# The narrow columns of a projection made with its first value block, in column groups of 296

## The chip, the cores and the metric

One core of one Trainium2 chip. The time is device microseconds of one execution; runs of the kernel before gave 530.16, 530.44 and 530.63 us, median 530.44. Lower is better.

## What is computed

A block of a streaming encoder, for 256 tokens of 2048 features, in float32. `h = RMSNorm(x)`; one projection `proj = h @ w_in` with 9296 columns, split into `qa ka va ga qb kb vb gb` (1024 columns each), `qi` (1024), and the two narrow ones: `ki` (64 columns, the indexer's key) and `wi` (16 columns, the indexer's head weights). Mixer A is chunked attention with a learned bias. Mixer B scores every key with an indexer,

```
logits = einsum('bqhd,bsd->bqhs', qi, ki);  score = einsum('bqh,bqhs->bqs', wi * idx_scale, relu(logits))
```

keeps the 64 best admissible keys of each query, and attends to these. Both outputs are gated by `silu(g)`, projected by `w_out`, added to `x`, and normed once more.

## The kernel before

Each float32 operand is split into a high part in the `f32r` format and the rest in the same format (`w_hi`, `w_lo`; `a_hi`, `a_lo`), and a product is made of three passes on TensorE: hi x hi, lo x hi, hi x lo. The RMS norm's scale is applied when results leave PSUM, so TensorE starts on `x * gain` before the sums of squares exist.

The weights stream in units of 256 rows (UK = 2 tiles k of 128) by 512 columns (512 KB) through a ring of four slots. For each unit the queue of SyncE (SP) issues a load once VectorE (DVE) has finished with the slot (`lo_done`), ScalarE (ACT) makes the high part (`split_hi`, L667 to 674) once TensorE (PE) has finished with the slot (`mm_done`), DVE the low part (`split_lo`, L956 to 961), and PE multiplies. 8 units are a block, 22 blocks the kernel. All orders are written out by hand, one instruction stream per engine.

There are two kinds of block. A token-major block (`unit`, L395) holds activations stationary and streams 512 weight columns: 96 matmuls of 512 columns, into two 512-column banks of `acc`, one for each tile m of 128 tokens. A feature-major block (`feature_unit`, L410) holds weights stationary and streams tokens: pairs of a matmul over hi and lo activations together (L426) and one with the low weights (L424 or L429). In blocks 1 and 2 it uses 192 of the 256 tokens, so the pairs are of 384 and 192 columns.

The stage that matters, in PE's order (L433 to L514): eight matmuls on zeros while the first loads fly; block 0, which is token-major and makes 512 columns of `va`, at first in halves of a unit (L442 to L479), each one k, so that PE can start early; units 0 to 2 of block 1 (feature-major, `qi`); the sums of squares, as matmuls with ones (L487 to L490); unit 3; the narrow columns, 80 of them stationary, 256 tokens moving, three passes for each of 16 k (L494 to L497) into `aux[0]`; a wait until block 0's result has left `acc` (`both_out(1)`, L499); units 4 and 5; three transposes that turn the narrow result token-major (L504 to L508); units 6 and 7; and two transposes of `ki_nat` (L512), which is the key normed and doubled. Block 2 (L542) then begins to need the indexer's keys.

The narrow weights, 640 KB, are one load (L301) with its own split (L734 on ACT, L1053 on DVE) into tiles `nw_raw`, `nw_hi`, `nw_lo`; the latter two serve later as scratch for attention. ACT squares the activations after its eighth split (L717 to L731), DVE adds them up between its low parts (L1034 to L1051), then makes the rates 1/rms per token in two layouts, `rstd` and `rk` (L1056 to L1062). `block_out` (L676 on ACT, L963 on DVE) takes block 0's result out of `acc`. On the queue of ACT lie the loads of the first activations and of the gain (L691, L692), on SP's the rest (L288 to L304).

Of the kernel before, what the change touches and what calls it, by code (L numbers as in the profile page):

```python
# [26 lines left out]
NARROW = IDX_D + IDX_H  # L27
QT = T - CHUNK
# [12 lines left out]
UK = 2  # L41
# [5 lines left out]
def hybrid_block(nc, xT, x, norm_gain, w_blocks, w_narrow, rel_bias, wo_blocks, final_gain, out):  # L47
# [7 lines left out]
    with ExitStack() as ctx:  # L55
# [10 lines left out]
        w_raw = sb("w_raw", [P, RING, UK * CB])  # L66
        w_hi = sb("w_hi", [P, RING, UK, CB], f32r)
        w_lo = sb("w_lo", [P, RING, UK, CB], f32r)
        nw_raw = sb("nw_raw", [P, KT * NARROW])
        nw_hi = sb("nw_hi", [P, KT, NARROW], f32r)  # L70
        nw_lo = sb("nw_lo", [P, KT, NARROW], f32r)
# [17 lines left out]
        narrow = sb("narrow", [NARROW, T])  # L89
        narrow_twice = sb("narrow_twice", [NARROW, P])  # L90
# [20 lines left out]
        idx_rate0 = sb("idx_rate0", [P, 1])  # L111
# [35 lines left out]
        nw_landed = sem("nw_landed")  # L147
# [16 lines left out]
        nhi_done = sem("nhi_done")  # L164
        nlo_done = sem("nlo_done")
# [5 lines left out]
        narrow_done = sem("narrow_done")  # L171
# [61 lines left out]
        AUX0_INDEX, AUX0_PAIRS = 2, 10  # L233
        AUX1_INDEX, AUX1_PAIRS = 2, 6
# [11 lines left out]
        w_hi4 = w_hi[:, :, :, :].rearrange("p r k c -> p r (k c)").rearrange("p r (k c) -> p r k c", k=2 * UK)  # L246
        w_lo4 = w_lo[:, :, :, :].rearrange("p r k c -> p r (k c)").rearrange("p r (k c) -> p r k c", k=2 * UK)

        nhi_flat, nlo_flat = flat(nw_hi[:, :, :]), flat(nw_lo[:, :, :])
# [21 lines left out]
        SCALAR_PART = slice(1408, D)  # L271

# [4 lines left out]
        def _(sp):  # L277
# [23 lines left out]
            sp.dma_start(nw_raw[:, :], w_narrow).then_inc(nw_landed, 16)  # L301
# [34 lines left out]
        def _(pool):  # L336
# [30 lines left out]
            pool.wait_ge(narrow_done, 1)  # L367
# [298 lines left out]
        def _(act):  # L666
# [33 lines left out]
            for u in range(HALVED):  # L700
                for kk in range(UK):
# [5 lines left out]
                    if k > 0:  # L707
                        a_part(k)
# [753 lines left out]
```

## Time and profile before

| | |
|---|---|
| median of three runs | 530.44 us (530.16 to 530.63) |
| the profiled execution's own time | 529.62 us |
| its span, first to last instruction | 527.6 us |
| PE busy | 519.2 us, 98% of the span |
| DVE, ACT, POOL busy | 366.7, 273.8, 29.8 us |
| granted TensorE clock | 0.997 of full speed |
| first matmul on data | 5.32 us |
| first matmul of block 1 | 27.67 us |
| first transpose of `ki_nat` | 52.73 us |

The span is what the trace covers; the time of an execution has some 2 us more around it. Times of single instructions are microseconds from the start of the span. A matmul's duration overlaps the next one's, so the price of a matmul in a stream is the distance from its start to the next start.

### The profile page before, as it was taken

The numbers are of one execution on the slowest core, as the hardware profiler recorded it, in microseconds if no ns is written. First come the engines' busy times: TensorE is split into PE (matmuls) and PEld (weight loads), VectorE is DVE, ScalarE is ACT, GpSimd is POOL, SyncE is SP. The second block draws the span as 40 slices with busy tenths as digits, with TensorE's granted clock in tenths as the row PEclk, the third lists the DMA queues.
The fourth block names the chain that finished last, engine by engine and source line by source line (L and its number), as shares of the span: only waits on it lengthen the run. The fifth ranks groups of instructions, "written<-read, shape, count | busy, mean of one in ns | idle before, by whom it ended". The sixth has DMA issues, their size and how long they took to land.

```text
span 527.6 us, 8251 instructions
## 1 busy us (share of the span) xinstructions
PE 519.2 (98%) x2871; PEld 451.9 (86%) x2871; DVE 366.7 (70%) x551; ACT 273.8 (52%) x405; POOL 29.8 (6%) x46
## 2 busy tenths in 40 slices
PE   9999999999999999999999999999999999999994
PEld 6899998888888888888888888888888888888883
DVE  6898685665668766767676767586877887646454
ACT  6875544444543344445554637374655566434342
POOL 1005043150000000000000000000000000000000
PEclk9999999999999999999999999999999999999998
DMA  8966966658555555563746454645555775665614
GB/s 298 381 205 187 288 203 214 196 174 279 172 190 196 197 199 183 182 196 106 234 145 194 148 176 157 191 147 183 159 160 176 252 250 170 189 198 194 202 44 159
DMA packets 72668, 102.53 MB, mean 194 GB/s; under 512 B 3504, under 2 KB 61760, under 8 KB 72384
## 3 DMA queue, kind: packets, MB, share of 16 engines
q1 hardware_dynamic: 70944, 96.68, 56.7%
q0 software_dynamic: 1264, 5.00, 3.0%
q10 hardware_dynamic: 432, 0.47, 0.3%
q8 instruction: 19, 0.31, 0.2%
q14 instruction: 9, 0.07, 0.1%
HBM read 99.24 MB, written 2.11 MB: 192 GB/s over the span
## 4 chain that ended last, share of the span: by engine, by line
PE 98%; DVE 0%; ACT 0%; DVEq 0%; issue 0%
PE acc L426 38%; PE acc L424 18%; PE acc L391 11%; PE acc L392 11%; PE acc L393 11%; PE acc L429 1%; PE aux L496 1%; PE acc L457 1%; PE aux L585 1%; PE aux L606 1%; PE acc L439 1%; PE aux L611 0%; PE aux L583 0%; PE aux L612 0%; PE aux L613 0%; PE aux L527 0%
## 5 line engine op out<-in xcount | busy, mean ns | idle before, releaser
L426 PE MATMUL acc<-acts,w_hi 128*128 128x512 f32 (+1 forms) x896 | 304.8, 389 | 0.0
L960 DVE TENSOR_TENSOR w_lo<-w_raw,w_hi 128x1024 fp32r<-128x1024 f32 x172 | 213.2, 1244 | 107.3 <-ACT w_hi L674 106.0
L674 ACT ACTIVATE w_hi<-w_raw 128x1024 fp32r<-128x1024 f32 x172 | 181.7, 1058 | 156.8 <-PE acc L426 81.9
L424 PE MATMUL acc<-acts,w_lo 128*128 128x256 f32 (+1 forms) x840 | 232.8, 277 | 0.0
L426 PEld LDWEIGHTS acc<-acts,w_hi 128*128 128x128 f32 x896 | 166.5, 188 | 30.1
L424 PEld LDWEIGHTS acc<-acts,w_lo 128*128 128x128 f32 x840 | 158.6, 189 | 1.0
L391 PE MATMUL acc<-w_hi,acts 128*128 128x512 f32 x248 | 96.6, 389 | 0.0
L392 PE MATMUL acc<-w_lo,acts 128*128 128x512 f32 x248 | 96.5, 389 | 0.0
L393 PE MATMUL acc<-w_hi,acts 128*128 128x512 f32 x248 | 96.5, 389 | 0.0
L391 PEld LDWEIGHTS acc<-w_hi,acts 128*128 128x128 f32 x248 | 46.6, 188 | 10.0 <-issue 0.3
L392 PEld LDWEIGHTS acc<-w_lo,acts 128*128 128x128 f32 x248 | 46.6, 188 | 9.6
L393 PEld LDWEIGHTS acc<-w_hi,acts 128*128 128x128 f32 x248 | 46.6, 188 | 9.6
L689 ACT ACTIVATE low<-acc 128x512 f32<-128x512 f32 (+1 forms) x28 | 16.0, 570 | 15.8 <-PE acc L426 15.8
L989 DVE TENSOR_TENSOR qk<-acc,low 128x512 f32<-128x512 f32 (+1 forms) x16 | 11.0, 687 | 9.2 <-ACT low L689 9.2
L383 POOL DMA_DIRECT2D qk<-x x1 | 0.5, 533 | 296.2 <-PE aux L585 296.2
L826 ACT ACTIVATE p<-p,neg_top,q_rate 128x256 f32<-128x256 f32 (+1 forms) x16 | 8.6, 537 | 15.9 <-DVE neg_top L1256 15.9
L429 PE MATMUL acc<-acts,w_lo 128*128 128x256 f32 (+1 forms) x56 | 15.5, 277 | 0.0
L829 ACT ACTIVATE p<-p,neg_max 128x256 f32<-128x256 f32 (+1 forms) x16 | 7.1, 444 | 11.8 <-DVE neg_max L1252 11.8
L924 ACT ACTIVATE t_gate<-z 128x512 f32<-128x512 f32 x8 | 5.0, 627 | 15.3 <-DVE z L1386 15.3
L835 ACT ACTIVATE nw_hi<-aux 128x512 fp32r<-128x512 f32 x8 | 4.8, 598 | 14.6 <-PE aux L597 14.6
L429 PEld LDWEIGHTS acc<-acts,w_lo 128*128 128x128 f32 x56 | 10.5, 188 | 1.1
L1129 DVE SCALAR_TENSOR_TENSOR iscore<-relu,w_idx,iscore 128x256 f32<-128x256 f32 x16 | 11.0, 688 | 0.3
(179 smaller groups left out, 388.1 us busy)
## 6 DMA issues: line engine op xcount, KB each, us to landing
w_raw<-w_blocks SPq DMA_DIRECT2D x140, 512.0 KB, 3.6
w_raw<-wo_blocks SPq DMA_DIRECT2D x32, 512.0 KB, 4.3
w_raw<-w_blocks SPq DMA_DIRECT2D x8, 256.0 KB, 5.3
qk<-x POOLq DMA_DIRECT2D x1, 2048.0 KB, 10.7
qk<-xT SPq DMA_DIRECT2D x7, 256.0 KB, 6.0
o<-ext_dram POOLq DMA_DIRECT2D x1, 1024.0 KB, 8.1
fgain<-final_gain POOLq DMA_DIRECT2D x1, 1024.0 KB, 7.8
out<-o SPq DMA_DIRECT2D x2, 512.0 KB, 3.0
```

The source lines that it names most:

```text
L391: nc.tensor.matmul(dst, a_hi[:, k, t], hi, start=start, stop=False)
L392: nc.tensor.matmul(dst, a_hi[:, k, t], lo, start=False, stop=False)
L393: return nc.tensor.matmul(dst, a_lo[:, k, t], hi, start=False, stop=stop)
L424: nc.tensor.matmul(acc[:, bank:bank + n], w_lo4[:, u % RING, q, c], a_hi[:, k, tokens], start=False, stop=False)
L426: last = nc.tensor.matmul(whole, w_hi4[:, u % RING, q, c], acts[:, k, :, tokens], start=(k == 0), stop=(k == KT - 1))
L429: nc.tensor.matmul(acc[:, bank:bank + n], w_lo4[:, u % RING, q, c], a_hi[:, k, tokens], start=False, stop=False)
L674: nc.scalar.activation(flat(w_hi[:, s, :, :]), w_raw[:, s, :], ACT.Copy).then_inc(hi_done, 1)
L689: nc.scalar.activation(low[:, half, :, 0:n], parts[:, :, n:2 * n], ACT.Copy).then_inc(low_out, 1)
L826: last = nc.scalar.activation(p[:, h, :], p[:, h, :], ACT.Exp, bias=neg_top[:, t, h:h + 1], scale=q_rate[:, 1 - t:2 - t], accum_out=p_sum[ ...
L960: nc.vector.tensor_tensor(flat(w_lo[:, s, :, :]), w_raw[:, s, :], flat(w_hi[:, s, :, :]).bitcast(f32), ALU.subtract).then_inc(lo_done, 1)
L989: nc.vector.tensor_tensor(dst, parts[:, :, 0:T], low[:, half, :, :], ALU.add).then_inc(feat_out, 1)
L1129: nc.vector.scalar_tensor_tensor(iscore1[:, :], relu1[:, h, :], w_idx1[:, head:head + 1], iscore1[:, :], ALU.mult, ALU.add).then_inc((isum ...
```

## The change

The 80 narrow columns are no longer a product of their own. They are appended to block 0's 512 columns: 592 columns for each k, made token-major as two groups of 296. The first group goes to `acc`, the second to `aux[0]` and `aux[1]` (for the two tiles of tokens), and holds the last 216 columns of `va` and the 80 narrow ones. The ring's slots are widened to 2 x 592 columns; other blocks use the first 1024 columns of a slot. The tiles `nw_raw`, `nw_hi`, `nw_lo`, `narrow` and `narrow_twice` go, and so do the 48 narrow matmuls and the three transposes. The scratch that later stages kept in `nw_hi` and `nw_lo` is now `parts_hi` and `parts_lo`.

The loads: 80 columns of two k are a load for each unit, with 320 bytes in a run; the first is on ACT's queue, the others ahead of their unit's weights on SP's. The first k's weights come in two pieces (296 and 216 columns), and are split and multiplied in two pieces. The sums of squares follow unit 0 of block 1 instead of unit 2; ACT and DVE make the squares and their sum correspondingly sooner, and `rstd` before `rk`. DVE reads the narrow columns directly from `aux`, just after it took the values out, and the transposes of `ki_nat` come after unit 5 instead of unit 7.

Loads, and PE's part:

```diff
+            def load_narrow(u):
+                sp.dma_start(raw_slots[:, u % RING, :].rearrange("p (k c) -> p k c", k=UK)[:, :, CB:WIDE],
+                             w_narrow[:, u * UK * NARROW:(u + 1) * UK * NARROW].rearrange("p (k c) -> p k c", k=UK)
+                             ).then_inc(nw_landed[u % RING], 16)
+
             for u in range(HALVED):
-                sp.dma_start(w_raw[:, u, 0:CB], w_blocks[VA_FIRST, u, :, 0:CB]).then_inc(half_landed[u], 16)
                 if u == 0:
+                    sp.dma_start(raw_slots[:, 0, 0:PART], w_blocks[VA_FIRST, 0, :, 0:PART]).then_inc(first_landed, 16)
+                    sp.dma_start(raw_slots[:, 0, PART:CB], w_blocks[VA_FIRST, 0, :, PART:CB]).then_inc(half_landed[0], 16)
                     sp.dma_start(xT_land[:, 1, :], xT[:, 1, :]).then_inc(xT_landed[0], 16)
-                sp.dma_start(w_raw[:, u, CB:2 * CB], w_blocks[VA_FIRST, u, :, CB:2 * CB]).then_inc(w_landed[u], 16)
+                else:
+                    load_narrow(u)
+                    sp.dma_start(raw_slots[:, u, 0:CB], w_blocks[VA_FIRST, u, :, 0:CB]).then_inc(half_landed[u], 16)
+                sp.dma_start(raw_slots[:, u, WIDE:WIDE + CB], w_blocks[VA_FIRST, u, :, CB:2 * CB]
+                             ).then_inc(w_landed[u], 16)
                 k = slice(UK * (u + 1), UK * (u + 2))
                 sp.dma_start(xT_land[:, k, :], xT[:, k, :]).then_inc(xT_landed[u + 1], 16)
             for u in range(HALVED, UNITS):
                 sp.wait_ge(lo_done, u - RING + 1)
-                load(u, w_blocks[VA_FIRST, u, :, :])
+                load_narrow(u)
+                sp.dma_start(raw_slots[:, u % RING, :].rearrange("p (k c) -> p k c", k=UK)[:, :, 0:CB],
+                             w_blocks[VA_FIRST, u, :, :].rearrange("p (k c) -> p k c", k=UK)
+                             ).then_inc(w_landed[u % RING], 16)
                 if u + 1 < UNITS:
                     k = slice(UK * (u + 1), UK * (u + 2))
                     sp.dma_start(xT_land[:, k, :], xT[:, k, :]).then_inc(xT_landed[u + 1], 16)
-            sp.dma_start(nw_raw[:, :], w_narrow).then_inc(nw_landed, 16)
...
+            def wide_pass(k, part, a, w, start=False, stop=False):
+
+                c = (k % UK) * WIDE + part * PART
                 for m in range(TM):
+                    dst = (acc[:, m * CB:m * CB + PART], aux[m][:, 0:PART])[part]
+                    last = nc.tensor.matmul(dst, a[:, k, m * P:m * P + P], w[:, (k // UK) % RING, c:c + PART],
+                                            start=start, stop=stop)
+                return last
...
+            wide_pass(0, 1, a_hi, lo_slots)
 
             for k in range(1, 2 * UK):
                 pe.wait_ge(ahi_done, k)
                 pe.wait_ge((half_hi, hi_done)[k % UK], k // UK + 1)
-                early_k(k, a_hi, w_hi)
+                for part in range(2):
+                    wide_pass(k, part, a_hi, hi_slots)
                 pe.wait_ge(alo_done, k + 1)
-                early_k(k, a_lo, w_hi)
+                for part in range(2):
+                    wide_pass(k, part, a_lo, hi_slots)
                 pe.wait_ge((half_lo, lo_done)[k % UK], k // UK + 1)
-                last = early_k(k, a_hi, w_lo)
...
+            for u in range(2, UNITS):
+                if u >= HALVED:
+                    pe.wait_ge(alo_done, UK * u + UK)
+                    pe.wait_ge(lo_done, u + 1)
                 for kk in range(UK):
                     k = u * UK + kk
-                    pe.wait_ge(alo_done, k + 1)
-                    pe.wait_ge((half_lo, lo_done)[kk], u + 1)
-                    for m in range(TM):
-                        last = mm3(acc[:, m * CB:m * CB + CB], k, m, w_hi[:, u, kk, :], w_lo[:, u, kk, :],
-                                   False, False)
+                    if u < HALVED:
+                        pe.wait_ge(alo_done, k + 1)
+                        pe.wait_ge((half_lo, lo_done)[kk], u + 1)
+                    for n, (a, w) in enumerate(((a_hi, hi_slots), (a_hi, lo_slots), (a_lo, hi_slots))):
+                        for part in range(2):
+                            last = wide_pass(k, part, a, w, stop=(k == KT - 1 and n == 2))
                 last.then_inc(mm_done, 1)
-            for u in range(HALVED, UNITS):
-                pe.wait_ge(alo_done, UK * u + UK)
-                unit(0, u)
-            for u in range(3):
-                feature_unit(1, u, 1, CHUNK)
+            feature_unit(1, 0, 1, CHUNK)
             pe.wait_ge(cleared, 3 + HEADS)
             pe.wait_ge(summed, UNITS)
             nc.tensor.matmul(aux[2][:, 0:T], ones_mat[:, :], x_sum[:, 0:T], start=True, stop=True)
             for m in range(TM):
                 last = nc.tensor.matmul(aux[3][:, m:m + 1], x_sum[:, m * P:m * P + P], ones[:, :], start=True, stop=True)
             last.then_inc(ssq_made, 1)
-            feature_unit(1, 3, 1, CHUNK)
-
-            pe.wait_ge(nlo_done, 1)
-            for k in range(KT):
-                for n, (w, a) in enumerate(((nw_hi, a_hi), (nw_hi, a_lo), (nw_lo, a_hi))):
-                    last = nc.tensor.matmul(aux[0][0:NARROW, 0:T], w[:, k, :], a[:, k, :],
-                                            start=(k == 0 and n == 0), stop=(k == KT - 1 and n == 2))
-            last.then_inc(narrow_done, 1)
+            for u in range(1, 4):
+                feature_unit(1, u, 1, CHUNK)
             both_out(1)
             feature_unit(1, 4, 1, CHUNK)
             feature_unit(1, 5, 1, CHUNK)
             pe.wait_ge(patterned, 1)
-            pe.wait_ge(aux_read[0], 1)
-            for m in range(TM):
-                nc.tensor.transpose(aux[1][:, m * P:m * P + NARROW], narrow[:, m * P:m * P + P],
-                                    ident[0:NARROW, 0:NARROW])
-            nc.tensor.transpose(aux[1][:, TM * P:TM * P + NARROW], narrow_twice[:, :],
-                                ident[0:NARROW, 0:NARROW]).then_inc(narrow_done, 1)
-            feature_unit(1, 6, 1, CHUNK)
-            feature_unit(1, 7, 1, CHUNK)
-            pe.wait_ge(aux_read[1], 2)
+            pe.wait_ge(aux_read[1], 1)
             for m in range(TM):
                 last = nc.tensor.transpose(aux[0][:, m * P:m * P + P], ki_nat[:, m, :], ident[:, :])
             last.then_inc(kit_done, 1)
+            feature_unit(1, 6, 1, CHUNK)
+            feature_unit(1, 7, 1, CHUNK)
```

ACT and DVE:

```diff
+            act.dma_start(raw_slots[:, 0, :].rearrange("p (k c) -> p k c", k=UK)[:, :, CB:WIDE],
+                          w_narrow[:, 0:UK * NARROW].rearrange("p (k c) -> p k c", k=UK)).then_inc(nw_landed[0], 16)
...
+                    c = WIDE_K[kk]
+                    if k == 0:
+                        act.wait_ge(first_landed, 16)
+                        nc.scalar.activation(hi_slots[:, 0, 0:PART], raw_slots[:, 0, 0:PART],
+                                             ACT.Copy).then_inc(first_hi, 1)
+                        c = slice(PART, WIDE)
                     act.wait_ge((half_landed, w_landed)[kk][u], 16)
+                    if kk == 0:
+                        act.wait_ge(nw_landed[u], 16)
...
             split_lo(0, 8)
-            for u in range(1, 4):
+            for u in range(1, 3):
                 add_square(u)
             split_lo(0, 9)
+            add_square(3)
             add_square(4)
-            add_square(5)
             split_lo(0, 10)
-            add_square(6)
-            split_lo(0, 11)
-            add_square(7)
+            for u in range(5, UNITS):
+                add_square(u)
             dve.wait_ge(summed, UNITS - 1)
             nc.vector.tensor_tensor(x_sum[:, 0:T], x_sum[:, 0:T], x_sum[:, T:2 * T], ALU.add).then_inc(summed, 1)
...
+            split_lo(0, 11)
             dve.wait_ge(ssq_made, 1)
```

DVE's order after that: `ssq`, `rk` (scaled), `split_lo(0, 12)`, `rstd`, the two rates, the values out of `acc` and `aux` in two pieces each (`acc_out` is given after the pieces of `acc`), `wi` and `ki_nat` from `aux`, `split_lo(0, 13)`, and then the reciprocals of `rk` and `q_rate`. ACT's: splits 8 to 12 with the squares, the roots of `ssq` and `rk`, the values in two pieces, split 13.

## Rows read from the trace of the kernel before

**Rows 1.** The page's busy times and chain: us (share) xinstructions; shares by engine.

```profile
PE 519.2 (98%) x2871; PEld 451.9 (86%) x2871; DVE 366.7 (70%) x551; ACT 273.8 (52%) x405; POOL 29.8 (6%) x46
...
PE 98%; DVE 0%; ACT 0%; DVEq 0%; issue 0%
```

**Rows 2.** Waits of PE over the span: us in total, times, longest.

```profile
PE acc L436 <- DVE ki_bd L998: 1.1, 1, 1.1
```

**Rows 3.** Timeline of PE, block 0: start us, us, what.

```profile
5.32 1.29 PE L444 MATMUL acc<-w_hi,acts 128*128 128x512 f32 x4
...
16.70 0.47 PE L391 MATMUL acc<-w_hi,acts 128*128 128x512 f32 x1
17.02 0.39 PE L392 MATMUL acc<-w_lo,acts 128*128 128x512 f32 x1
...
27.67 0.33 PE L426 MATMUL acc<-acts,w_hi 128*128 128x384 f32 x1
```

**Rows 4.** Chain of waits, 0 to 60 us: start, us, what.

```profile
34.77 0.43 PE aux L487 x2
...
37.93 5.58 PE aux L496 x48
```

**Rows 5.** Timeline of PE around the three transposes, block 1.

```profile
47.71 0.37 PE L426 MATMUL acc<-acts,w_hi 128*128 128x384 f32 x1
...
48.09 0.33 PE L424 MATMUL acc<-acts,w_lo 128*128 128x192 f32 x1
48.26 0.36 PE L426 MATMUL acc<-acts,w_hi 128*128 128x384 f32 x1
```

**Rows 6.** Timeline of PE, matmuls of 256 columns in a row (attention scores).

```profile
236.63 0.28 PE L581 MATMUL aux<-nw_hi 128*128 128x256 f32 x1
...
237.34 0.27 PE L585 MATMUL aux<-qk,q_early 128*128 128x128 f32 x1
```

**Rows 7.** Timeline of PE, a pair of 384 and 192 columns.

```profile
28.32 0.36 PE L426 MATMUL acc<-acts,w_hi 128*128 128x384 f32 x1
28.52 0.25 PE L424 MATMUL acc<-acts,w_lo 128*128 128x192 f32 x1
28.61 0.37 PE L426 MATMUL acc<-acts,w_hi 128*128 128x384 f32 x1
```

**Rows 8.** Timeline of all engines, the start.

```profile
4.91 0.35 DVE L1003 TENSOR_SCALAR acts<-qk,gain 128x256 fp32r<-128x256 f32 x1 [3.48 <-DMA gain<-norm_gain]
6.83 0.51 ACT L696 ACTIVATE acts<-qk,gain 128x256 fp32r<-128x256 f32 x1 [0.81 <-DMA qk<-xT]
...
14.24 1.06 ACT L674 ACTIVATE w_hi<-w_raw 128x1024 fp32r<-128x1024 f32 x1 [0.28 <-DMA w_raw<-w_blocks]
```

**Rows 9.** Issues of DMAs: KB each, us to landing.

```profile
gain<-norm_gain ACTq DMA_DIRECT2D x1, 8.0 KB, 3.7
```

**Rows 10.** DMA queues, 0 to 5, 5 to 20, 20 to 45 us: packets, MB, share of 16 engines.

```profile
q10 hardware_dynamic: 288, 0.14, 11.2%
...
q1 hardware_dynamic: 2472, 5.80, 102.7%
...
q1 hardware_dynamic: 5345, 5.49, 69.2%
```

**Rows 11.** Groups of DVE and of ACT, to 28 us: busy us, mean ns.

```profile
L1018 DVE TENSOR_TENSOR w_lo<-w_raw,w_hi 128x512 fp32r<-128x512 f32 x8 | 5.5, 689 | 0.4 <-ACT w_hi L710 0.4
L960 DVE TENSOR_TENSOR w_lo<-w_raw,w_hi 128x1024 fp32r<-128x1024 f32 x6 | 7.3, 1225 | 1.8 <-ACT w_hi L674 1.8
...
L710 ACT ACTIVATE w_hi<-w_raw 128x512 fp32r<-128x512 f32 x8 | 5.0, 626 | 1.6 <-DMA w_raw<-w_blocks 1.5
```

**Rows 12.** Timeline of DVE: three sums of squares, the last sum, values out.

```profile
25.45 2.28 DVE L1038 TENSOR_TENSOR o<-o 128x512 f32<-128x512 f32 x3
...
33.78 0.43 DVE L1051 TENSOR_TENSOR o<-o 128x256 f32<-128x256 f32 x1
...
41.28 0.75 DVE L966 TENSOR_SCALAR v<-acc,rstd 128x512 f32<-128x512 f32 x1
```

More of the change, by code:

```diff
@@ L27 @@
 NARROW = IDX_D + IDX_H
+WIDE = CB + NARROW
+PART = WIDE // 2
+V_REST = CB - PART
 QT = T - CHUNK
@@ L146, in hybrid_block @@
         xT_landed = [sem(f"xT_landed{c}") for c in range(UNITS)]
-        nw_landed = sem("nw_landed")
+        first_landed = sem("first_landed")
+        nw_landed = [sem(f"nw_landed{s}") for s in range(RING)]
         gain_landed = sem("gain_landed")
@@ L673, in split_hi @@
                     act.wait_ge(mm_done, g * UNITS + (c - RING + 1))
-                nc.scalar.activation(flat(w_hi[:, s, :, :]), w_raw[:, s, :], ACT.Copy).then_inc(hi_done, 1)
+                nc.scalar.activation(hi_slots[:, s, 0:UK * CB], w_raw[:, s, :], ACT.Copy).then_inc(hi_done, 1)
             def block_out(g, dst):
@@ L1066, in _ @@
                                            ALU.mult).then_inc(rated, 1)
-            dve.wait_ge(rated, 2)
+            dve.wait_ge(mm_done, UNITS)
+            nc.vector.tensor_scalar(v1_flat[:, V_COLUMNS[0]], acc[:, CB:CB + PART], rstd[:, 1:2], None,
+                                    ALU.mult).then_inc(acc_out[1], 1)
+            nc.vector.tensor_scalar(v1_flat[:, V_COLUMNS[1]], aux[1][:, 0:V_REST], rstd[:, 1:2], None, ALU.mult)
+            dve.wait_ge(v_hi_done, 1)
+            for part, (c, src) in enumerate(zip(V_COLUMNS, (acc[:, 0:PART], aux[0][:, 0:V_REST]))):
+                last = nc.vector.scalar_tensor_tensor(v0_lo_flat[:, c], src, rstd[:, 0:1], v0_hi_flat[:, c].bitcast(f32),
+                                                      ALU.mult, ALU.subtract)
+                if part == 0:
+                    last.then_inc(acc_out[0], 1)
+            dve.wait_ge(rated, 2)
+            nc.vector.tensor_scalar(w_early[:, :], aux[0][:, V_REST + IDX_D:PART], idx_rate[:, 0:1], None,
+                                    ALU.mult).then_inc(w_scaled, 1)
+            nc.vector.tensor_scalar(w_idx1[:, :], aux[1][:, V_REST + IDX_D:PART], idx_rate[:, 1:2], None, ALU.mult)
+            for m in range(TM):
+                for h in range(2):
+                    last = nc.vector.tensor_scalar(ki_nat[:, m, h * IDX_D:(h + 1) * IDX_D],
+                                                   aux[m][:, V_REST:V_REST + IDX_D], rstd[:, m:m + 1], None, ALU.mult)
+            last.then_inc(aux_read[1], 1)
+            dve.wait_ge(w_scaled, 1)
+            for f in range(2):
+                nc.vector.tensor_copy(w_idx0[rows[f], :, :],
+                                      w_early[CHUNK:P, :].rearrange("p (i f h) -> p i f h", i=4, f=2)[:, :, f, :])
+            split_lo(0, 13)
+            dve.wait_ge(std_done, 2)
+            nc.vector.reciprocal(rk[:, :], rk[:, :]).then_inc(rk_made, 1)
             nc.vector.reciprocal(q_unit[:, :], q_rate[:, :]).then_inc(rated, 1)
-            for h in range(2):
-                nc.vector.tensor_copy(idx_rate0[rows[h], :], idx_rate[CHUNK:P, 0:1]).then_inc(rated, 1)
-            split_lo(0, 13)
-            block_out(0, 1, slice(2 * CB, 3 * CB))
             split_lo(0, 14)
@@ L1082, in _ @@
             split_lo(0, 17)
-            dve.wait_ge(rated, 5)
-            dve.wait_ge(narrow_done, 2)
-            early_w = aux[1][:, TM * P + IDX_D:TM * P + NARROW].rearrange("p (i f h) -> p i f h", i=4, f=2)
-            for f in range(2):
-                nc.vector.tensor_scalar(w_idx0[rows[f], :, :], early_w[rows[f], :, f, :], idx_rate0[rows[f], :], None,
-                                        ALU.mult)
-            nc.vector.tensor_scalar(w_idx1[:, :], aux[1][:, P + IDX_D:P + NARROW], idx_rate[:, 1:2], None, ALU.mult)
-            for m in range(TM):
-                for h in range(2):
-                    last = nc.vector.tensor_scalar(ki_nat[:, m, h * IDX_D:(h + 1) * IDX_D],
-                                                   aux[1][:, m * P:m * P + IDX_D], rstd[:, m:m + 1], None, ALU.mult)
-                last.then_inc(aux_read[1], 1)
-            split_lo(0, 18)
             dve.wait_ge(kit_done, 1)
```

123 lines of the change are left out of this document (64 added, 59 removed).

## The prediction, before the changed kernel was run

> **What bounds the kernel now.** I read the busy times and the chain first [rows 1]. PE is busy for 98% of the span and the chain that ended last runs on PE for 98% of it, while DVE, ACT and the queues have next to none. The list of PE's waits over the whole span has one entry, 1.1 us before any data is there [rows 2]. So a change pays exactly what it takes from PE's stream, and costs what it makes PE wait. No other engine's saving counts by itself. The timeline of PE then gives the price of each kind of matmul, as the distance from start to start.
>
> - 512 columns: block 0 is 96 matmuls. Its 50th starts at 17.02 us and block 1 starts at 27.67 [rows 3], which is 47 matmuls later, so 0.2266 us each.
> - 256 columns: six in a row from 236.63 to 237.34 [rows 6], 0.118 us each.
> - The 48 narrow matmuls, 80 columns stationary and 256 moving: 5.58 us [rows 4], 0.116 us each.
> - In block 1 a matmul of 384 columns holds the next one off for 0.20 us and one of 192 for 0.09 [rows 7].
>
> Block 0 takes 27.67 - 5.32 = 22.35 us [rows 3]; 96 x 0.2266 is 21.75, so 0.60 us of it are start-up: late operands in the first units, and at 16.70 a matmul that holds the next off for 0.32 instead of 0.23 after a late low part.
>
> **What goes.** Block 0, 22.35 us, and the narrow matmuls, 5.58 us. The three transposes: between a 384 matmul and the 192 after it lie 47.71 and 48.09, 0.38 us where 0.20 is usual, and the next start comes 0.17 later instead of 0.09 [rows 5, 7], together 0.26 us. Sum 28.19 us. The sums of squares (0.43 us and a little more, rows 4), the two transposes of `ki_nat` and all feature units stay in the stream and only change places: nothing on either side.
>
> **What comes.** 16 k x 3 passes x 2 token tiles x 2 groups = 192 matmuls of 296 columns. No row has 296 columns. The line through the points at 256 and 512 gives 0.118 + 40 x (0.2266 - 0.118)/256 = 0.135 us. Bounds from other rows: below, no less than the 256-column price, 0.118. Above, the line from 256 to the 384 columns of block 1, 0.118 + 40 x (0.20 - 0.118)/128 = 0.1436. I take 0.135: the straight line through 256 and 512 gives 0.172 at 384, so the 0.20 is a price of that mixed pair, and for a row of equal matmuls the evidence is the 256s and 512s. 192 x 0.135 = 25.92 us; by the bounds 22.7 and 27.6.
>
> **Start-up.** PE starts at 5.32 because `a_hi[0]` is made when the gain lands at 4.91 [rows 8]. That does not move, since gain and the first activations are issued first as before. The first piece of weights is smaller and lands no later than the 4.2 us of now, so that first pass is not late, but it was not what PE waited for: the two-piece load by itself brings at most a tenth or two. What is new is ACT's wait for the first narrow load before it may split the second piece. It is issued third on ACT's queue, 0.45 us behind the gain (from about 1.65), and with the gain's 3.7 us to landing [rows 9] it arrives at 5.4. Behind that waiting instruction on ACT are `a_hi[1]` and the high part of k 1, and DVE's second low piece follows it. ACT: second piece 5.4 to 5.85; `a_hi[1]` to 6.3; high part of k 1 (592 columns, 626 ns x 592/512 = 0.72, rows 11) to 7.0. PE meanwhile has group 0 (hi x hi), then waits for group 1 until 5.9, and goes through 12 matmuls to about 7.3. Unhindered they would have ended at 6.94. With some 0.3 us for the first matmuls, which today already come slower than the rest, I put the new start-up at 0.7 us beside the 0.60 now. Bounds: 0.3 if the load lands by 5.0, 1.8 if it lands at 6.5, where each tenth counts one for one.
>
> After that PE takes 12 x 0.135 = 1.62 us for a k and 3.24 for a unit, where it took 1.36 and 2.72. For a k, DVE needs 0.80 us for the low part (689 ns x 592/512, rows 11) and some 0.5 for the activations, ACT 0.72 and 0.51 [rows 8, 11]: both hidden. The DMA engines, full at 102.7% from 5 to 20 us [rows 10], are the nearer limit. Packets: 5.80 MB in 2472 packets at 102.7% of 15 us x 16 is 100 ns for 2.35 KB; 5.49 MB in 5345 at 69.2% of 25 x 16 is 52 ns for 1.03 KB; the line through both puts a packet of 320 B at 26 ns, the short packets of q10 at 31 ns on the mean [rows 10]. A unit's narrow part is 256 packets, so 256 x 26/16 = 0.42 us of all engines. Ahead of the weights of unit 4 lie five such loads, 2.1 us. Today they land at 14.24 [rows 8], then at 16.4; high part 1.23 us (1.06 x 1184/1024), low part 1.42 (1.225 x 1184/1024, rows 11), ready at 19.0. PE arrives at unit 4 at 5.32 + 0.7 + 4 x 3.24 = 18.98. So unit 4 has no slack at all, just as now, and a tenth or two of wait is within my 0.7. In the units before, the loads shift by 0.4 to 1.7 us (the activations of unit 1, waited for until 6.83 in rows 8, come at 7.3 or so; PE needs them at 9.2), and PE's slower pace covers that. From unit 5 on a unit's loads take 0.42 us longer than now and PE takes 0.52 us longer, so the queue keeps its place or gains.
>
> A rule of the Trainium skill speaks against these loads: "DMA: Bandwidth & Descriptors", under Specifications, asks for at least 512 B in a transfer for full rate and says that below it the engine reads, modifies and writes. The q10 row, where more than half of the packets are short, does not show that, but it holds no data packet between 64 and 1024 B. If a packet of 320 B cost twice as much, see the second rival.
>
> **Behind block 0.** Block 1 begins at 5.32 + 0.7 + 25.92 = 31.94. Unit 0 takes 8 x 0.289 = 2.31 us [rows 7], so PE wants the sum of squares at 34.25. ACT's split 10 waits for PE's seventh unit, 28.7, and ends at 29.8; DVE's low part to 31.0, three additions 2.28 us, the last one 0.43 [rows 12]: 33.7, ahead by 0.5 us. This is the shortest slack of the tail. Then both sums are on PE until 35.0. `rstd` waits on DVE behind low part 12 (1.22 us, from about 35.6 on), and is there at about 37; the values in two pieces for each tile, some 0.45 us for 296 columns by the 0.75 us for 512 [rows 12], let `acc` go by 38.6. PE reaches `both_out(1)` after three units of 2.31 us, at 41.9: 3 us of cover, where the narrow product gave it before. The reads of `ki_nat` and the head weights, seven short operations, lie before low part 13, which is then done at 41.2 and wanted at 44.2. `ki_nat`'s transposes at 46.6 find it ready and leave DVE more time before block 2 than now. POOL's removed wait was met long before the features it also waits for. From block 2 on nothing is different but the slots' pitch, and PE was never short there: the gain of the stage is kept to the end.
>
> **Sum.** 28.19 - (25.92 + 0.7) = 1.57 us. The profiled execution took 529.62 us around its span of 527.6: with the change 528.05. The median of the runs shown is 0.82 us higher than that execution, so on the median's scale 530.44 - 1.57 = 528.87, and I say 528.9.
>
> **Rivals.** (1) The 296-column matmul costs 0.1436 us, by the dearer line: 192 x 0.1436 = 27.57, and the gain is -0.1 us, time 530.5. For: block 1's rows show that smaller matmuls do not always follow the straight line. Against: 256 in a row cost 0.118, so 296 would have to leap. (2) Short packets cost double, 52 ns: 2.1 us more before unit 4, which then waits 2.1 us: gain -0.5, time 531.0. For: full DMA engines at that very place, and the rule named above. Against: q10's short packets at 31 ns. (3) Slower: the first narrow load lands very late. Its descriptors share the DMA engines with 1.2 MB on SP's queue, and loads behind a full queue have taken some 6 us. The mechanism is ACT's wait at the start, for which all splits queue up. It decides from a landing at 5.4 + 1.57 + 1.06 = 8.0 us on; at 8.3 the time is 530.44 - 1.57 + 2.9 = 531.8. For: full engines from 2.5 us on. Against: the gain, directly ahead in the same queue, took 3.7 us. (4) The sum of squares is late after all and PE waits in front of it: its slack is 0.5 us, and a DVE 1.2 us later than I have it costs 0.7: time 529.6, within the noise.
>
> **Chances.** A change of 0.2%, 1.06 us, is about what can be told from none; the borders are 529.4 and 531.5. Forecast 0.66 (own range 527.6 to 529.4), rival 1 0.09, rival 2 0.10, rival 3 0.06, rival 4 0.09. Rivals 1, 2 and 4 are no change. That makes faster 0.67, same 0.26, slower 0.07. The low end is a price of 0.130 us and a start-up of 0.5: 28.19 - 25.5 = 2.7, so 527.7; the high end reaches to rival 1, 530.5.
>
> **What the profile after would show.** 192 matmuls of 296 columns, 0.135 us from start to start; block 1's first matmul at 31.9 us; no narrow product; transposes of `ki_nat` near 46.7; block 2's first matmul 1.6 us earlier than now; no entry in PE's waits at the sum of squares or at `both_out(1)`. The second split on ACT begins at 5.4. I am wrong if the pitch is off by more than 0.005 us (a microsecond), if PE's first twelve matmuls last past 8 us, or if unit 4 waits for its low part for more than a few tenths.

## The result: slower, and the profile after

Before 530.30 us (median of 6, 529.82 to 530.63), after 534.21 (6 runs, 533.99 to 534.77); ratio 1.0077 [1.0066, 1.0087]. The forecast was 528.9 with a range to 530.5. The change costs 3.9 us instead of bringing 1.6. The profiled execution of the changed kernel took 534.77 us, its span is 532.6: 5.0 us more than before [rows 1]. That pair is 1.1 us wider apart than the medians: the profiled execution before lies 0.7 us under its median, the one after 0.6 over. The terms below, read from the two traces, are held against 5.0.

The page's busy times and its chain, against [rows 1]. PE is still the whole chain; 1% of DMA is new.

```profile
PE 522.6 (98%) x2916; PEld 457.7 (86%) x2916; DVE 366.7 (69%) x552; ACT 273.6 (51%) x404; POOL 30.2 (6%) x46
...
PE 97%; DMA 1%; DVE 0%; ACT 0%; ACTq 0%; issue 0%; DVEq 0%
```

All waits of PE over the span (us in total, times, longest), against [rows 2]. One is new, and it is not among those of the sums of squares or of the block's end.

```profile
PE aux L465 <- ACT hi_slots L732: 1.5, 1, 1.5
PE acc L454 <- DVE ki_bd L1020: 1.1, 1, 1.1
```

Where it arises: timeline of PE, ACT and DVE at the start (start us, duration us, what, in brackets the idle time before and its releaser), against [rows 3, 8].

```profile
4.79 0.35 DVE L1025 TENSOR_SCALAR acts<-qk,gain 128x256 fp32r<-128x256 f32 x1 [3.37 <-DMA gain<-norm_gain]
...
5.20 0.54 PE L465 MATMUL acc<-hi_slots,acts 128*128 128x296 f32 x2
...
6.73 0.45 ACT L732 ACTIVATE hi_slots<-raw_slots 128x296 fp32r<-128x296 f32 x1 [2.10 <-DMA raw_slots<-w_narrow]
...
7.24 0.55 PE L465 MATMUL aux<-hi_slots,acts 128*128 128x296 f32 x2 [1.50 <-ACT hi_slots L732]
```

ACT may split the second piece only when the narrow load is there, and that is at 6.73, not at 5.4. PE stands for 1.50 us. The later timeline of PE has a second loss, then the steady pace, and the end of the block:

```profile
7.90 0.46 PE L465 MATMUL aux<-hi_slots,acts 128*128 128x296 f32 x2
8.18 0.68 PE L465 MATMUL acc<-lo_slots,acts 128*128 128x296 f32 x2
...
9.14 0.70 PE L465 MATMUL acc<-hi_slots,acts 128*128 128x296 f32 x2
9.64 0.70 PE L465 MATMUL aux<-hi_slots,acts 128*128 128x296 f32 x2
...
11.61 0.44 PE L465 MATMUL aux<-lo_slots,acts 128*128 128x296 f32 x2
...
20.05 0.44 PE L465 MATMUL acc<-hi_slots,acts 128*128 128x296 f32 x2
20.33 0.43 PE L465 MATMUL aux<-hi_slots,acts 128*128 128x296 f32 x2
...
34.77 0.34 PE L444 MATMUL acc<-acts,hi_slots 128*128 128x384 f32 x1
```

From 9.14 to 9.64 two matmuls take 0.50 us, at 20 us two take 0.27 to 0.28. The granted clock explains it. The busy time of each engine in three stretches (us, PE, PEld, DVE, ACT, POOL with instruction counts, granted clock, DMA share, GB/s):

```profile
7.00:8.00 1.00, 0.76 (x5) 0.77 (x6) 0.79 (x2) 1.00 (x3) 0.00 (x0) 1.00 1.04 365
8.50:9.50 1.00, 1.00 (x6) 1.00 (x5) 1.00 (x3) 1.00 (x3) 0.00 (x0) 0.50 1.08 378
12.00:13.00 1.00, 1.00 (x10) 1.00 (x9) 1.00 (x3) 0.99 (x3) 0.00 (x0) 1.00 1.03 393
```

The clock is at its upper level (2.4 GHz) until 8.17 us, at the lower (1.2 GHz) to 11.58, and at the upper again. Ahead of the fall PE had idled 1.50 us. The Trainium skill, "TensorE: Matmul & The Clock Gate", Part 1, puts an idle array at the lower clock; the trace agrees with the direction. By the mean granted clocks on record not every execution fell. In all thirteen traces the clock is also at the lower level for 1.9 to 4.7 us behind PE's last matmuls; with 3.41 us at half on top the mean can reach at most 0.995, as in two of the six executions (534.77 and 534.47). The other four, 533.99 to 534.33, have 0.996 or 0.997. (0.995 alone proves no fall; kernels that had none in their traces show it at times.) By this estimate the median of the changed kernel is one without the fall.

Block 0 now takes 34.77 - 5.20 = 29.57 us, where 26.62 was forecast and 28.19 replaced. That is 3.0 of the missing 6.6 us (the 5.0 lost and the 1.6 not gained). The rest is where the forecast had put nothing. Timeline of PE in a later block, three starts of a unit, 12 matmuls of 512 columns apart:

```profile
192.56 0.40 PE L409 MATMUL acc<-hi_slots,acts 128*128 128x512 f32 x1
...
195.35 0.39 PE L409 MATMUL acc<-hi_slots,acts 128*128 128x512 f32 x1
...
198.08 0.40 PE L409 MATMUL acc<-hi_slots,acts 128*128 128x512 f32 x1
```

The first unit takes 2.79 us and the next 2.73: 232.7 and 227.9 ns a matmul, counted in the trace's ns. Before, all took 226.7. I call the distance from one start to the next the pitch. Over all 671 token-major matmuls behind block 0 the mean pitch is 230.3 ns, 226.7 before: 2.4 us. For the 840 matmuls of the features' low pass (720 of 256 columns, 120 of 192) it is 116.3 against 114.4: 1.6 us. For the 896 of the high pass it is 226.9 against 227.4: -0.5. Together 3.5 us. Seen as groups (line, shapes, count, busy us, mean ns), after and then before:

```profile
L442 PE MATMUL acc<-acts,lo_slots 128*128 128x256 f32 x720 | 204.2, 284 | 0.0
...
L411 PE MATMUL acc<-hi_slots,acts 128*128 128x512 f32 x224 | 88.0, 393 | 0.0
```

```profile
L424 PE MATMUL acc<-acts,w_lo 128*128 128x256 f32 x720 | 202.4, 281 | 0.0
...
L393 PE MATMUL acc<-w_hi,acts 128*128 128x512 f32 x248 | 96.5, 389 | 0.0
```

3 or 4 ns in the mean of one, in a row without a single wait. What differs is the place of the operands: a slot is 1184 float32 wide instead of 1024, so slots 1 and 3 begin 128 B off a multiple of 256 B. (All such offsets are counted from the first ring's start; its absolute address is not on record.) The sum: -1.57 (forecast) + 2.95 (block 0) + 3.5 = 4.9 of the 5.0.

### The profile page after: what moved, and what is told of

It reads as the page before. It is cut to its first block, busy times and chain, and to the rows that moved or that the text cites. A ratio compares the mean times of both kernels' runs of the same rounds, so it can differ in the third digit from the quotient of the medians.

```text
span 532.6 us, 8352 instructions
## 1 busy us (share of the span) xinstructions
PE 522.6 (98%) x2916; PEld 457.7 (86%) x2916; DVE 366.7 (69%) x552; ACT 273.6 (51%) x404; POOL 30.2 (6%) x46
## 4 chain that ended last, share of the span: by engine, by line
PE 97%; DMA 1%; DVE 0%; ACT 0%; ACTq 0%; issue 0%; DVEq 0%
PE acc L444 38%; PE acc L442 18%; PE acc L411 10%; PE acc L410 10%; PE acc L409 10%; PE aux L465 3%; PE acc L465 3%; PE acc L447 1%; DMA raw_slots<-w_narrow 1%; PE aux L597 1%; PE aux L618 1%; PE aux L537 0%; PE aux L623 0%; PE aux L624 0%; PE aux L593 0%; PE aux L625 0%
## 5 line engine op out<-in xcount | busy, mean ns | idle before, releaser
L444 PE MATMUL acc<-acts,hi_slots 128*128 128x512 f32 (+1 forms) x896 | 305.2, 389 | 0.0
L982 DVE TENSOR_TENSOR lo_slots<-raw_slots,hi_slots 128x1024 fp32r<-128x1024 f32 x168 | 208.0, 1242 | 108.8 <-ACT hi_slots L686 107.5
L686 ACT ACTIVATE hi_slots<-raw_slots 128x1024 fp32r<-128x1024 f32 x168 | 177.4, 1058 | 160.7 <-PE acc L444 81.0
L442 PE MATMUL acc<-acts,lo_slots 128*128 128x256 f32 (+1 forms) x840 | 234.8, 279 | 0.0
L444 PEld LDWEIGHTS acc<-acts,hi_slots 128*128 128x128 f32 x896 | 166.9, 188 | 29.4
L442 PEld LDWEIGHTS acc<-acts,lo_slots 128*128 128x128 f32 x840 | 158.8, 189 | 1.1
L411 PE MATMUL acc<-hi_slots,acts 128*128 128x512 f32 x224 | 88.0, 393 | 0.0
L409 PE MATMUL acc<-hi_slots,acts 128*128 128x512 f32 x224 | 87.9, 393 | 0.0
L410 PE MATMUL acc<-lo_slots,acts 128*128 128x512 f32 x224 | 87.9, 393 | 0.0
L410 PEld LDWEIGHTS acc<-lo_slots,acts 128*128 128x128 f32 x224 | 42.1, 188 | 9.6
L411 PEld LDWEIGHTS acc<-hi_slots,acts 128*128 128x128 f32 x224 | 42.1, 188 | 9.5
L409 PEld LDWEIGHTS acc<-hi_slots,acts 128*128 128x128 f32 x224 | 42.1, 188 | 9.4
L447 PE MATMUL acc<-acts,lo_slots 128*128 128x256 f32 (+1 forms) x56 | 15.5, 277 | 0.0
```

The lines of the kernel that those rows point to most:

```text
L409: nc.tensor.matmul(dst, a_hi[:, k, t], hi, start=start, stop=False)
L410: nc.tensor.matmul(dst, a_hi[:, k, t], lo, start=False, stop=False)
L411: return nc.tensor.matmul(dst, a_lo[:, k, t], hi, start=False, stop=stop)
L442: nc.tensor.matmul(acc[:, bank:bank + n], w_lo4[:, u % RING, q, c], a_hi[:, k, tokens], start=False, stop=False)
L444: last = nc.tensor.matmul(whole, w_hi4[:, u % RING, q, c], acts[:, k, :, tokens], start=(k == 0), stop=(k == KT - 1))
L447: nc.tensor.matmul(acc[:, bank:bank + n], w_lo4[:, u % RING, q, c], a_hi[:, k, tokens], start=False, stop=False)
```

## The experiments

Two suspects, taken one at a time and then together: where the slots begin, and how block 0 starts. Each run's ratio is to the kernel before on the same chip (its medians there 530.16 to 530.26).

### Where the slots begin

**The kernel before, its three rings at 1056 float32 a slot** (slots 1 and 3 start 128 B off 256):

```diff
...
-        w_hi = sb("w_hi", [P, RING, UK, CB], f32r)
+        w_hi = sb("w_hi", [P, RING, 1056], f32r)[:, :, 0:UK * CB].rearrange("p r (k c) -> p r k c", k=UK)
...
```

> The kernel before, with 1056 instead of 1024 float32 in each slot of the three rings (raw, high, low), so that slots 1 and 3 start 128 B off a multiple of 256 B, as in the changed kernel; nothing else is changed. Theory (where a slot starts sets the price of a matmul): token-major matmuls go from 226.7 to about 232 ns in odd units, and the time rises by about 3 us, to 533. Rival (the slower matmuls come from the changed loads or the changed order): no difference, 530.3 us.

533.52 us, ratio 1.007 [1.0053, 1.0087]. Nothing but the slots' start was changed. By unit the pitch alternates between 227.9 and 232.6 ns, as three starts of a unit show, and the groups read as in the changed kernel:

```profile
199.73 0.39 PE L391 MATMUL acc<-w_hi,acts 128*128 128x512 f32 x1
...
202.47 0.40 PE L391 MATMUL acc<-w_hi,acts 128*128 128x512 f32 x1
...
205.26 0.39 PE L391 MATMUL acc<-w_hi,acts 128*128 128x512 f32 x1
```

```profile
L424 PE MATMUL acc<-acts,w_lo 128*128 128x256 f32 x720 | 203.9, 283 | 0.0
...
L393 PE MATMUL acc<-w_hi,acts 128*128 128x512 f32 x248 | 97.4, 393 | 0.0
```

**The changed kernel with slots of 1216 float32** (4864 B, 19 x 256; `bias_ext` laid into `fgain` to make room):

```diff
...
-        hi_slots = sb("hi_slots", [P, RING, UK * WIDE], f32r)
+        hi_slots = sb("hi_slots", [P, RING, 1216], f32r)[:, :, 0:UK * WIDE]
...
```

> The changed kernel with 1216 float32 in a slot instead of 1184, so that every slot starts on a multiple of 256 B (a small tile is laid into another to make room). Theory of the slots' start: all later blocks go back to 226.7 ns in token-major and 114.4 for the low matmul, about 3.3 us less, 530.9 us. Rival: 534.2 us as before, with the matmuls at 230 ns.

531.54, ratio 1.0025 [1.0015, 1.0035]: two thirds of the loss are gone, 2.7 us of the 3.5 that the slots account for. Its profiled execution stood for 1.81 us at the start, not 1.50, and its clock was at the lower level from 8.80 to 12.21 us. Every unit behind block 0 takes 226.7 ns a matmul again, and the low pass 114.3:

```profile
L442 PE MATMUL acc<-acts,lo_slots 128*128 128x256 f32 x720 | 202.4, 281 | 0.0
...
L411 PE MATMUL acc<-hi_slots,acts 128*128 128x512 f32 x224 | 87.1, 389 | 0.0
```

Three more sizes, all on the kernel before, say which boundary counts and whose reads. **All rings at 1088** (4352 B, 17 x 256):

> The kernel before with 1088 float32 in each slot, so that each slot starts on a multiple of 256 B, but slots 1 and 3 on no multiple of 512 B (a small tile is laid into another to make room). Theory A (256 B is the boundary that matters): 226.7 ns for a token-major matmul and 530.2 us. Theory B (any pitch that is no power of two, or no multiple of 512 B, costs): 229 to 232 ns and about 533 us.

530.20 us, ratio 1.0003 [0.9994, 1.0013]; the low pass back at 202.4 us busy:

```profile
L424 PE MATMUL acc<-acts,w_lo 128*128 128x256 f32 x720 | 202.4, 281 | 0.0
...
L393 PE MATMUL acc<-w_hi,acts 128*128 128x512 f32 x248 | 96.5, 389 | 0.0
```

**Only the raw ring at 1056**, which ACT and DVE read and the DMAs write, and PE never touches:

> The kernel before with 1056 float32 in a slot of the raw ring alone; PE's operands (high and low rings) start where they did. Theory (PE's own reads are dearer from a start 128 B off): nothing changes, 530.2 us. Rival (DMA, ACT and DVE work slower on misplaced slots and disturb PE): token-major matmuls at about 230 ns, and about 533 us.

530.20 us, ratio 1.0 [0.9991, 1.001], the pitch 226.7. So the price hangs on the two rings that PE reads. ACT writes one of them, and DVE writes and reads them; no run shifts PE's reads without these. But the price goes with the slot that PE is reading at the time, so I take it to be PE's reads.

**All rings at 1040**, so that the slots begin 0, 64, 128 and 192 B off:

> The kernel before with 1040 float32 in each slot of all three rings: slot 1 starts 64 B, slot 2 128 B, slot 3 192 B off a multiple of 256 B. If any start off 256 B costs the same, units 1, 2, 3 of each four are at about 232 ns and the time is about 535 us (three slow slots instead of two); if only the parity of 128 B counts, slot 2 alone is slow and the time is near 531.8.

535.54 us, ratio 1.0103 [1.0087, 1.012]. By slot: 228.4, 230.3, 232.9 and 232.9 ns; the low pass 116.6. Three of four slots pay now. The busy time of the low group, 204.1 us, hardly differs from the 203.9 with two slots off; only the pitch shows the difference.

So a matmul of 512 columns whose operand starts at a multiple of 256 B follows the last one after 226.7 ns, 64 B off after 230.3, 128 or 192 B off after 232.9. Slot 0, which is never off, also takes 1.2 to 1.7 ns more while the others are. The trace shows where: with slots 1 and 3 off, the first three matmuls on slot 0 take 231.9, 231.5 and 230.2 ns, and the nine others 226.7. So the extra stands right behind the slot that is off and is gone a few matmuls later.

### How block 0 starts

**The idle time filled.** To hold the clock up, seven matmuls with zeros into a bank not in use, behind the first pass of group 0:

```diff
             wide_pass(0, 0, a_hi, hi_slots, start=True)
+            for _ in range(7):
+                nc.tensor.matmul(aux[2][:, 0:CB - HD // 2], ki_bd[:, 0, 0:P], zeros, start=True, stop=True)
```

> The changed kernel with seven matmuls of zeros (448 columns, into a bank that is not yet used) between PE's first pass over group 0 and its wait for group 1, so that PE is busy in those 1.5 us; the wait itself stays. Theory (the idle time let the clock fall to 1.2 GHz from about 8.2 to 11.6 us, and that cost about as much as the wait): the granted clock stays at its full level and the time falls by 1.5 to 1.9 us, to 532.5. Rival (only the wait costs): no change or slightly slower, 534.2 to 534.4.

536.51 us, ratio 1.0124 [1.0108, 1.0141]. Each took 0.70 us, more than I had taken, and the row runs on past the operand's arrival; the clock stayed up, but the total, 2.3 us above the changed kernel where 1.7 less was expected, says nothing on the clock's price:

```profile
5.20 5.42 PE L473 MATMUL aux<-ki_bd 128*128 128x448 f32 x14
10.11 0.78 PE L465 MATMUL aux<-hi_slots,acts 128*128 128x296 f32 x2
```

**Three instead of seven:**

> As the kernel with seven zero matmuls, but with three: in that run one of them took 0.70 us and the seven overshot the wait by 3 us. Three take 2.1 us and end at about 7.3, where the wait ended anyway. Theory (the wait cost its own length and then a stretch at 1.2 GHz): the clock stays up, block 0 ends 1.6 to 1.8 us sooner than in the changed kernel; of that up to 1.5 us may be lost again in front of the sums of squares, which DVE finishes at about 36.9, so 532.5 to 534 us. Rival (the clock falls all the same, or costs nothing): block 0 lasts 29.6 us as in the changed kernel.

534.22 us, ratio 1.0083 [1.0066, 1.01]: the same as without. But the trace separates the clock's share. The fill ends 0.8 us after the time at which PE had gone on by itself, and the clock does not fall after it:

```profile
5.57 2.98 PE L473 MATMUL aux<-ki_bd 128*128 128x448 f32 x6
8.04 0.78 PE L465 MATMUL aux<-hi_slots,acts 128*128 128x296 f32 x2
```

```profile
5.00:10.00 5.00, 5.00 (x21) 3.60 (x21) 3.25 (x7) 3.21 (x7) 0.00 (x0) 1.00 1.01 348
10.00:15.00 5.00, 5.00 (x39) 5.00 (x38) 4.73 (x10) 4.41 (x10) 0.00 (x0) 1.00 1.07 386
```

(The first records of the fill are still slow, 948 ns at 5.57 us against 540 from 6.88 on, though the view says 1.00: the clock rose for the first time only then.) From group 1's start to block 1 it is 34.27 - 8.04 = 26.23 us, without the fill 34.77 - 7.24 = 27.53: the low clock costs 1.3 us of block 0. The fill starts the rest 0.8 us late, and block 1 comes 0.5 us sooner. PE keeps that lead: it takes the sums at 36.74, without an entry in its waits, and the profiled execution took 534.04 us against 534.77.

```profile
PE acc L454 <- DVE ki_bd L1022: 1.1, 1, 1.1
```

The medians are level. That fits the estimate above, by which most executions of the changed kernel had no fall to be spared; no run tests it.

**The narrow columns in one row with the block's,** 592 columns laid side by side in HBM, so that there is no narrow load, no short packet and no wait for one:

```diff
-                    load_narrow(u)
-                    sp.dma_start(raw_slots[:, u, 0:CB], w_blocks[VA_FIRST, u, :, 0:CB]).then_inc(half_landed[u], 16)
-                sp.dma_start(raw_slots[:, u, WIDE:WIDE + CB], w_blocks[VA_FIRST, u, :, CB:2 * CB]
-                             ).then_inc(w_landed[u], 16)
+                    sp.dma_start(raw_slots[:, u, 0:WIDE], w_wide[u, :, 0:WIDE]).then_inc(half_landed[u], 16)
+                sp.dma_start(raw_slots[:, u, WIDE:2 * WIDE], w_wide[u, :, WIDE:2 * WIDE]).then_inc(w_landed[u], 16)
...
-                    if kk == 0:
-                        act.wait_ge(nw_landed[u], 16)
```

> The changed kernel with the narrow columns laid beside the value columns in DRAM, so that each unit is one load of 592 columns a k (the first k in two pieces of 296), and no separate narrow loads exist; slots as in the changed kernel. Theory (late first narrow load, then the fallen clock): wait and slow clock both go, block 0 lasts 26.2 us and a few tenths instead of 29.6, and the time is about 531.0. Rival (ACT would be late anyway at the start, or the loads are late by their bytes): at most 1.5 us gained, 532.7 or more.

534.15 us, ratio 1.0078 [1.0062, 1.0095]: no gain, against what I expected. The start went better: block 0 from 4.81 to 32.55, 27.74 us where 26.2 "and a few tenths" was expected, with one wait of 0.7 us and no fall of the clock. Then PE gives it back. Its waits, and the rows around the sum of squares:

```profile
PE aux L500 <- DVE o L1065: 1.7, 1, 1.7
PE acc L454 <- ACT hi_slots L717: 0.7, 1, 0.7
```

```profile
34.66 0.36 PE L433 MATMUL acc<-acts,hi_slots 128*128 128x384 f32 x1
...
36.11 0.43 DVE L1065 TENSOR_TENSOR o<-o 128x256 f32<-128x256 f32 x1
...
36.68 0.67 PE L500 MATMUL aux<-o,ones_mat 128*128 128x256 f32 x2 [1.66 <-DVE o L1065]
```

PE idles 1.66 us there, longer than the 1.50 at the changed kernel's start, and the clock stays up. In the changed kernel the sum is 0.5 us later still, and nobody sees it, because PE itself comes late:

```profile
36.60 0.42 DVE L1081 TENSOR_TENSOR o<-o 128x256 f32<-128x256 f32 x1
...
36.88 0.36 PE L444 MATMUL acc<-acts,hi_slots 128*128 128x384 f32 x1
...
37.17 0.67 PE L511 MATMUL aux<-o,ones_mat 128*128 128x256 f32 x2
```

One late thing had covered another: block 1 starts 2.2 us sooner with the joined loads, the sums 0.5. What makes DVE late is upstream of it: ACT splits units 4 to 7 at 16.17, 18.46, 20.80 and 24.34, each after a wait for its load, where before it did at 14.24, 16.20, 18.16 and 20.11. The last of them:

```profile
24.34 1.19 ACT L741 ACTIVATE hi_slots<-raw_slots 128x1184 fp32r<-128x1184 f32 x1 [1.55 <-DMA raw_slots<-w_blocks]
```

These loads go at the pace of the DMA engines, which are full (shares of 1.07 from 10 to 25 us): 1.96 us a unit before, 2.3 now, and that is the growth from unit 4 to unit 6. Unit 7 takes 3.5. Just before it lands, the DMA queues from 20 to 24 us hold one packet that belongs to no load of the program, instructions, 16 KB:

```profile
q8 instruction: 1, 0.02, 1.7%
```

It starts at 21.64 us and takes 1.09 us of its DMA engine's time, where a packet of 2048 B takes 0.08. With the joined loads it comes at 19.50, and there unit 6 is the one that takes 3.65 us (18.07 to 21.72); in the kernel before it comes at 24.86, behind block 0's loads. No run moves this packet alone, so that it causes the delay is likely and not shown.

### Together, and the rest of the waits

**Joined loads and slots of 1216:**

> The changed kernel with both corrections: each unit's 592 columns a k in one load, and slots of 1216 float32, on multiples of 256 B. With the joined loads alone block 0 began at 4.81 and block 1 at 32.55, but PE then stood 1.7 us in front of the sums of squares. Theory (three separate losses: late first load with the fallen clock, slots, sums too early): the slots' 3.3 us come back, the wait at the sums stays: 530.9 us. Rival (the wait at the sums was an accident of that run): 529.2.

529.99 us, ratio 0.9994 [0.9985, 1.0004]: level with the kernel before, 0.9 us better than expected, and 4.2 below the joined loads alone where the slots account for 3.5. PE waits 1.5 us at the sums and 0.6 for ACT.

**And the sums of squares on PE one unit later,** behind unit 1 of block 1:

```diff
             feature_unit(1, 0, 1, CHUNK)
+            feature_unit(1, 1, 1, CHUNK)
             pe.wait_ge(cleared, 3 + HEADS)
```

> As e8, with the sums of squares after unit 1 of block 1 instead of after unit 0. Theory: DVE has the sum at about 36.5 us and PE comes to it at about 36.9, so nothing waits there nor at the values out of acc (about 41.3 against 42.3): 529.2 us, 1.0 us below the kernel before. Rival (the wait only moves on to both_out(1), or to the transposes): 530.9 as without it.

529.51 us, ratio 0.9988 [0.9979, 0.9997]. The wait at the sums is gone, 1.3 us are left at the start:

```profile
PE acc L454 <- ACT hi_slots L718: 1.3, 2, 0.7
```

**And the first k's weights in one piece again,** one load and one split on ACT and on DVE instead of two:

```diff
-                    sp.dma_start(raw_slots[:, 0, 0:PART], w_wide[0, :, 0:PART]).then_inc(first_landed, 16)
-                    sp.dma_start(raw_slots[:, 0, PART:WIDE], w_wide[0, :, PART:WIDE]).then_inc(half_landed[0], 16)
+                    sp.dma_start(raw_slots[:, 0, 0:WIDE], w_wide[0, :, 0:WIDE]).then_inc(half_landed[0], 16)
```

> As e9, with the first k's 592 columns in one load, one high part and one low part. Prices the two-piece start by itself. Theory (PE waits for a_hi[0], not for the weights, so the pieces bring a tenth or two): 0.1 to 0.4 us more than e9, not to be told from it. Rival (the pieces are worth the better part of a microsecond, as one load of 592 columns lands and is split later than the gain arrives): 0.7 us or more above e9.

528.64 us (9 runs, 528.40 to 529.62), ratio 0.9969 [0.9959, 0.9979], 0.87 us better than with two pieces, and eight of the nine lie under the lowest of the two-piece kernel (528.99): I had the sign wrong. Its waits of PE, then the first matmuls and block 1's first:

```profile
PE acc L442 <- DVE ki_bd L999: 1.1, 1, 1.1
PE aux L526 <- issue: 0.2, 1, 0.2
```

```profile
5.25 0.81 PE L453 MATMUL acc<-hi_slots,acts 128*128 128x296 f32 x2
...
32.09 0.34 PE L432 MATMUL acc<-acts,hi_slots 128*128 128x384 f32 x1
```

PE starts 0.37 us later than with two pieces (4.88), has no entry for ACT in its waits, and reaches block 1 0.78 us sooner (32.09 against 32.87). What the extra load costs stands in SP's own timeline, k 1's second load in the one-piece and then in the two-piece kernel:

```profile
1.67 0.43 SPq L300 DMA_DIRECT2D raw_slots<-w_wide  x1
```

```profile
2.14 0.43 SPq L301 DMA_DIRECT2D raw_slots<-w_wide  x1
```

A DMA issued there moves the next ones by 0.47 us, in the stretch in which ACT waits for each. The load itself lands 0.3 us sooner (6.32 against 6.64). That this issue is the whole price is argued, not shown: the split and the first matmuls changed with it. This kernel beats both.

| kernel | us | ratio to before |
|---|---|---|
| after | 534.21 | 1.0077 |
| after, slots at 256 B | 531.54 | 1.0025 |
| joined loads, slots at 256 B | 529.99 | 0.9994 |
| the same, sums one unit later | 529.51 | 0.9988 |
| the same, first weights in one piece | 528.64 | 0.9969 |

## Why the prediction was wrong

**The failed step** is the last one behind block 0: "From block 2 on nothing is different but the slots' pitch, and PE was never short there: the gain of the stage is kept to the end." PE was indeed never short. But the pitch of the slots is itself a price on every matmul that reads them: 3.5 us over the kernel, by the trace, and 3.4 by the same shift made in the kernel before (533.52 against 530.16). I read "PE waits for nothing" as "PE's instructions cost what they did".

**The start-up term, sized 0.7 us,** is the second. Block 0 takes 29.57 us; 192 x 0.1363 are 26.17, so start-up is 3.4. Of it 1.50 are idle and 1.3, in the profiled execution, the low clock after it. Of the other 0.6, half is the first two matmuls, which take 0.54 us from start to idle instead of 0.27, and half lies behind 7.24, where the kernel with three fills has it too (26.23 against 190 x 0.1363 = 25.90). The landing at 5.4 rested on the gain's 3.7 us [rows 9], 8 KB in the same queue. The narrow load is 80 KB in 320 B packets beside SP's traffic and took 5.0 us. My bound of 1.8 was for a landing at 6.5 without the clock; by its rule of one for one 6.73 would have given 2.0, and the clock comes on top.

**The two-piece load** was put at "a tenth or two" of gain. In the joined kernel it costs 0.9 us. I counted the smaller piece's earlier landing and put the issue that it adds on SP at nothing.

**The sum of squares, slack 0.5 us,** comes at 37.0 and not 33.7. I had unit 4's loads right (16.4 forecast, ACT begins at 16.17), but "From unit 5 on ... the queue keeps its place or gains" is wrong: the splits fall from 1.9 us behind the kernel before at unit 4 to 4.2 at unit 7. I set 0.42 us more for the loads against 0.52 more for PE, but the loads weren't waiting for PE: in the kernel before they came every 1.96 us and PE used them every 2.72. So 0.3 to 0.4 us more a unit goes straight into the splits. Rival 4 is thus true of the changed kernel, hidden there by PE's own delay, and costs 1.7 us where that is taken away.

**Right:** the pitch of a 296-column matmul (0.1363 us against 0.135, so not rival 1); the 28.19 us that go (with them the sum closes to 0.1 us), and the moved pieces at nothing: no wait at `both_out(1)` nor at `ki_nat`'s transposes. Short packets did not cost double, so rival 2 fell too: by their medians those of 320 B took 20 ns (2048 of them), of 1024 B 46 and of 2048 B 84, all on one line. The rule on transfers under 512 B, in the Trainium skill's "DMA: Bandwidth & Descriptors", Specifications, is not seen in this load. Rival 3, a very late narrow load, had the mechanism of the start-up right but was set to decide from 8.0 us on.

The idea of the stage holds: with the slots at 256 B, joined loads, one first piece and the sums a unit later, block 0 takes 32.09 - 5.25 = 26.84 us, forecast 26.62, and the kernel gains 1.58 us by its medians, forecast 1.57. That these two agree to the hundredth is luck: by the stage's own sum it should be 28.19 - 26.84 = 1.35, and a median has a spread of a few tenths.

**Open:** why PE's reads are dearer off 256 B; whether the instruction packet causes the late unit; when the clock falls (1.50 us of idle time did it at the start, 1.66 us at 35 us did not); and how much of the start's price the executions without the fall pay.

## What to carry to other kernels

Where PE is the bound, a buffer's new width is part of the change: keep the start of whatever PE reads at a multiple of 256 B, and compare the mean of an unchanged matmul before and after before looking for waits. A stall of PE at the start may cost the clock behind it too, and each DMA put ahead of others on a queue is priced with its issue. When a removed delay brings nothing, look for the next late thing that it had covered.

## What the runs showed of the hardware

- Matmuls of 512 columns in `f32r`, 128 x 128 stationary, from start to start: 226.7 ns with the ring's operand at a multiple of 256 B, 230.3 at 64 B off, 232.9 at 128 or 192 B off. 256 moving columns against stationary ring weights, mean over the slots: 118.3 to 118.4 and, with slots off, 120.6 to 120.9. Shifting only the ring that PE does not read cost nothing (ratio 1.0 [0.9991, 1.001]). The aligned slot behind one that is off pays for its first matmuls (231.9, 231.5, 230.2 ns, then 226.7).
- After 1.50 us without work, ended at 7.24 us, the granted clock was at its lower level from 8.17 to 11.58 us, which cost 1.3 us of block 0, nearly as much as the idle time. After 1.81 us, ended at 7.47, it was there from 8.80 to 12.21. After 1.66 us, ended at 36.68 in the kernel with joined loads, it did not fall.
- At the start the zero matmuls run at the lower level, 954 ns a record against 540; the clock first rises between 4.0 and 6.7 us, and where differs from one execution to the next.
- Matmuls with zeros of 448 columns in plain float32 took 0.70 us each at the upper level (seven in 4.91 us), and leave two records each in the trace.
- A DMA's issue on SP holds the next off for 0.44 to 0.47 us at the start (0.76, 1.20, 1.67, 2.14).
- An instruction packet of 16 KB took 1.09 us on a DMA engine (at 21.64 us in the changed kernel).
